# A two-block network on one core: four weight slots instead of three, split in place, and four pieces ahead of the norm's factor

## The chip, the cores and the metric

The kernel runs on one core of a Trainium2 chip. TensorE (PE) does the matrix products, ScalarE (ACT) and VectorE (DVE) the elementwise work, GpSimd (POOL) splits the weights into two parts, and SyncE (SP) only issues the weight loads. The metric is the device time of one execution in microseconds (us), lower is better.

## The reference, cut to what matters

Two blocks of two layers each work on the same 512 tokens of width 1024, all in float32.

```python
def rms_norm(x, g):                      # also _rmsnorm of the second block
    y = xf * lax.rsqrt(jnp.mean(xf * xf, axis=-1, keepdims=True) + RMS_EPS)
    return (y * g.astype(jnp.float32)).astype(x.dtype)

def first_block(x, ...):                 # x is 512 tokens x 1024
    for layer in range(2):
        h = rms_norm(x, norm_mix_pre[layer])
        if layer % 2 == 0:               # qkv: 1024 -> 9216, 3 groups of 8 heads, then 1024 -> 1024
            h = dilated_attention_mixer(h, attn_w_qkv[j], attn_w_o[j], rel_bias)
        else:                            # 1024 -> 2048, conv of 4 taps, gates, a scan over tokens, 1024 -> 1024
            h = rglru_mixer(h, lru_w_in[j], lru_conv_w[j], ..., lru_w_out[j])
        x = x + rms_norm(h, norm_mix_post[layer])
        h = rms_norm(x, norm_ffn_pre[layer])
        h = conv_ffn(h, ffn_w_up[layer], ffn_conv_w[layer], ffn_conv_b[layer], ffn_w_down[layer])
        x = x + rms_norm(h, norm_ffn_post[layer])
    return x

def conv_ffn(x, w_up, conv_w, conv_b, w_down):      # 1024 -> 6144 -> 3072 -> 1024
    u = causal_dwconv(x @ w_up, conv_w, conv_b)
    g, v = u[..., :D_FF], u[..., D_FF:]
    return (jax.nn.gelu(g, approximate=True) * v) @ w_down

def second_block(x, mem, norm_g, ...):
    for l in range(2):
        z = _rmsnorm(x, norm_g[l]) @ w_in[l]        # then split into the inputs of three branches
        o_a = _nsa(...) * silu(nsa_silu)            # compressed, selected and window attention
        o_b = _fox(...) * silu(fox_silu)
        o_m = _memory_xattn(mem_q, _rmsnorm(mem, mem_norm_g[l]) @ w_mem_kv[l], ...) * silu(mem_silu)
        u = sum over the three branches of sigmoid(merge_g) * (o @ w_branch)
        x = x + u @ w_out[l]
    return x
```

## The kernel before

**Weights.** All weights lie in memory as 434 units of 128 x 1024 floats (512 KB), in the order in which PE wants them (`unit_order`). A unit goes through three engines. SP loads it into `w_raw` of one of `SLOTS` slots. POOL rounds it into `w_hi` (L2002) and writes the rest, w_raw - w_hi, into `w_lo` in four quarters (L2006). PE then multiplies it in `pe_unit` (L355 to L357): 8 tiles, and for each tile w_hi by the high part of the activations, w_hi by their low part, and w_lo by the high part, which is 24 matmuls of 512 columns. Before the change there are three slots, each with its own `w_raw`, `w_hi` and `w_lo`. SP loads unit u as soon as POOL has split unit u-3 (L2016), and POOL splits unit u once it is loaded and PE has finished unit u-3 (L2001).

**Stages.** The program is a row of stages: the attention of the first block (its start runs on `order[0:3]`), the output projection `attn_out`, ffn 0, the recurrent stage (lru), ffn 1, and then, for two layers, the projections `z` of the second block, its attentions, and the merge. Six stages begin with a norm (`pe_norm_start`, L413): the activations enter unscaled, units 0 and 1 of the stage are multiplied together, chunk by chunk, as the chunks come from ACT and DVE, and PE sums the squares beside it (L393). After that DVE works out the norm's factor by twelve small instructions on 128x4 numbers (`dve_rsqrt`, L460 to L475), PE multiplies unit 2, and then PE spreads the factor over all partitions (`pe_norm_spread`, L408, L399), ACT copies it (L446, `factor_wide`), and only now can the banks of units 0, 1 and 2 be evicted by DVE, with the factor in the multiplication.

**Between stages.** Four stages (ffn 0, lru, ffn 1 and the first `z`) begin with the norm of what came before (`pe_post_begin`, L426): the last unit's bank is squared, PE sums it (L393), DVE finds the factor by the same twelve instructions into `narrow`, PE spreads it (L399), DVE scales eight chunks (L509), and POOL adds each to the residual `x_res` (`pool_post`, L520, L523). The place of `pool_post` in POOL's order is set by the table `post` in `pool_program` (L1996): it stands behind the split of unit SLOTS - 1 of the new stage.

**Order within a stage.** Each engine's order is written out by hand, and each waits on counters of the others. In lru, DVE has for each of eight units an eviction (L1007), three taps of the convolution (L1014) and the low part (L991), while PE goes on with the next units; the second group of gates waits for the eviction of the last one. In `z` the work beside unit m is listed by `later` (L1103): at m = 1 a rotation matmul (L1179) of what was evicted from unit 0, at m = 3 the gates' transposes (L1192), which want the eviction of unit 2 and a sigmoid.

## Time and profile before

| | us |
|---|---|
| median of 3 timed runs | 3247.79 |
| lowest and highest | 3241.72, 3254.14 |
| the profiled execution, its own time | 3239.93 |
| its span, from the first to the last instruction | 3238.5 |
| granted TensorE clock, mean of the span | 0.973 |

The profile is of one execution. Its span is the time between its first and last instruction, and 1.4 us of its own time lie outside. The busy time of PE is modelled from pipelined matmuls, so its share is no measure of how near PE is to its limit: idle time before an instruction, with what ended it, is read in its place. A clock of 1 is 2.4 GHz and 0.5 is 1.2 GHz.

### The profile page before, as it was taken

What the parts mean: (1) busy time and instruction counts of PE and PEld (TensorE: products, weight loads), DVE (VectorE), ACT (ScalarE), POOL (GpSimd) and SP (SyncE); (2) the same over time, 40 slices, a digit from 0 to 9 for tenths busy, and PEclk for the clock granted to TensorE, in tenths of its full rate; (3) what the DMA queues carried; (4) which work ended last, traced back from release to release, by engine and by line L of the source; (5) the groups of instructions that cost most, each with busy time, mean ns of one, the idle gap of its engine ahead of it and who ended that gap; (6) DMA issues with size and microseconds to landing.
All of it is one profiled execution on the core that took longest, in us unless ns stands there. A gap on an engine that the chain in (4) does not pass through costs nothing.

```text
span 3238.5 us, 41911 instructions
## 1 busy us (share of the span) xinstructions
PE 3068.2 (95%) x15410; PEld 2538.1 (78%) x15410; DVE 1541.2 (48%) x3162; ACT 820.7 (25%) x1763; POOL 1903.9 (59%) x2206
## 2 busy tenths in 40 slices
PE   7999999899998888999989999999999999999999
PEld 6888887678887667888877777778887787777887
DVE  2333334377721684777035745553233654655232
ACT  1111111222211342222012125553111213555110
POOL 5555554588877677898764751115775573111775
PEclk9999999899999999999999999999999999999999
DMA  3222221122222212222322220001233221000232
GB/s 143 89 92 83 90 101 59 53 91 98 98 98 85 65 65 73 97 98 98 110 92 98 85 78 21 27 21 66 98 117 107 70 89 55 27 22 26 85 98 91
DMA packets 66873, 255.71 MB, mean 79 GB/s; under 512 B 7664, under 2 KB 8176, under 8 KB 64880
## 3 DMA queue, kind: packets, MB, share of 16 engines
q1 hardware_dynamic: 62496, 227.57, 21.0%
q10 hardware_dynamic: 4176, 25.47, 2.2%
q8 instruction: 125, 2.05, 0.3%
q14 instruction: 76, 0.62, 0.1%
HBM read 250.91 MB, written 2.10 MB: 78 GB/s over the span
## 4 chain that ended last, share of the span: by engine, by line
PE 87%; DVE 8%; ACT 2%; issue 2%; DMA 0%; POOL 0%; ACTq 0%; DVEq 0%; POOLq 0%
PE bank L355 21%; PE bank L357 21%; PE bank L356 21%; PE bank L1692 4%; PE bank L1666 2%; PE bank L1677 2%; PE bank L393 2%; PE bank L383 1%; PE bank L621 1%; PE bank L1661 1%; PE bank L385 1%; PE bank L384 1%; PE bank L1424 1%; PE bank L593 1%; PE bank L1164 1%
## 5 line engine op out<-in xcount | busy, mean ns | idle before, releaser
L2006 POOL TENSOR_TENSOR w_lo<-w_raw,w_hi 128x256 fp32r<-128x256 f32 x1736 | 1383.6, 828 | 36.2
L2002 POOL TENSOR_SCALAR w_hi<-w_raw 128x1024 fp32r<-128x1024 f32 x434 | 474.9, 1094 | 1257.6 <-PE bank L357 1128.5
L355 PE MATMUL bank<-in_hi,w_hi 128*128 128x512 f32 x1408 | 555.6, 395 | 5.7 <-ACT factor_wide L446 2.8
L357 PE MATMUL bank<-in_hi,w_lo 128*128 128x512 f32 x1408 | 549.4, 390 | 0.0
L356 PE MATMUL bank<-in_lo,w_hi 128*128 128x512 f32 x1408 | 549.1, 390 | 0.0
L355 PE MATMUL bank<-z_hi,w_hi 128*128 128x512 f32 x976 | 394.5, 404 | 0.0
L357 PE MATMUL bank<-z_hi,w_lo 128*128 128x512 f32 x976 | 384.2, 394 | 0.0
L356 PE MATMUL bank<-z_lo,w_hi 128*128 128x512 f32 x976 | 383.6, 393 | 0.0
L355 PEld LDWEIGHTS bank<-in_hi,w_hi 128*128 128x128 f32 x1408 | 265.3, 188 | 59.9 <-ACT factor_wide L446 3.5
L357 PEld LDWEIGHTS bank<-in_hi,w_lo 128*128 128x128 f32 x1408 | 264.9, 188 | 55.5
L356 PEld LDWEIGHTS bank<-in_lo,w_hi 128*128 128x128 f32 x1408 | 265.3, 188 | 53.1
L357 PEld LDWEIGHTS bank<-z_hi,w_lo 128*128 128x128 f32 x976 | 185.2, 190 | 40.4
L355 PEld LDWEIGHTS bank<-z_hi,w_hi 128*128 128x128 f32 x976 | 185.7, 190 | 39.0 <-POOL w_lo L2006 1.0
L356 PEld LDWEIGHTS bank<-z_lo,w_hi 128*128 128x128 f32 x976 | 185.7, 190 | 38.7 <-issue 2.0
L1775 DVE TENSOR_REDUCE at_st<-bank 128x1 f32<-128x256 f32 (+4 forms) x288 | 118.7, 412 | 171.6 <-PE bank L1667 101.6
L575 DVE TENSOR_TENSOR out_squares<-out_squares,square 128x512 f32<-128x512 f32 x32 | 32.6, 1019 | 279.1 <-ACT square L566 279.0
L1705 ACT ACTIVATE at_pt<-bank 128x256 f32<-128x256 f32 (+4 forms) x288 | 112.2, 390 | 198.6 <-PE bank L1677 194.2
L355 PE MATMUL bank<-ffn_hidden_hi,w_hi 128*128 128x512 f32 x384 | 149.4, 389 | 0.0
L356 PE MATMUL bank<-ffn_hidden_lo,w_hi 128*128 128x512 f32 x384 | 149.4, 389 | 0.0
L357 PE MATMUL bank<-ffn_hidden_hi,w_lo 128*128 128x512 f32 x384 | 149.4, 389 | 0.0
L1677 PE MATMUL bank<-ident,at_p 128*128 128x128 f32 (+1 forms) x608 | 120.6, 286 | 24.2 <-ACT at_p L1712 23.8
L1712 ACT ACTIVATE at_p<-bank,at_st,nsa_scale 128x31 f32<-128x31 f32 (+2 forms) x192 | 103.2, 537 | 41.7 <-DVE at_st L1786 39.3
(427 smaller groups left out, 5157.2 us busy)
## 6 DMA issues: line engine op xcount, KB each, us to landing
w_raw<-in_units SPq DMA_DIRECT2D x434, 512.0 KB, 3.4
bias<-in_bias ACTq DMA_DIRECT2D x8, 1152.0 KB, 5.0
o_all<-in_cmp_w ACTq DMA_DIRECT2D x4, 2048.0 KB, 8.5
x_res<-in_x ACTq DMA_DIRECT2D x4, 512.0 KB, 9.0
mem_in<-in_mem ACTq DMA_DIRECT2D x2, 1024.0 KB, 4.8
out<-x_res ACTq DMA_DIRECT2D x4, 512.0 KB, 2.6
consts<-in_consts ACTq DMA_DIRECT2D x1, 710.5 KB, 3.7
both_layers_cols<-in_layer_cols ACTq DMA_DIRECT2D x2, 140.5 KB, 4.7
```

What stands on the lines that cost most here:

```text
L355: pe.matmul(out, hi[:, w], rh, start=start and n == 0, stop=False)
L356: pe.matmul(out, hi[:, w], rl, start=False, stop=False)
L357: last = pe.matmul(out, lo[:, w], rh, start=False, stop=stop and n == len(tiles) - 1)
L393: m = pe.matmul(bank[:, t:t + 1], sq[:, t * P:t * P + P], c.ones[:, 0:1], start=first and t == 0, stop=last, skip_group_check=True)
L1666: pe.matmul(b[:, 0:t.keys], c.nsa_q[:, t.n, q], k[:, 0:t.keys], start=True, stop=False)
L1677: m = pe.matmul(b[0:t.rows, s * P:s * P + P], p[:, s * P:s * P + t.rows], c.ident[:, :], is_transpose=True)
L1692: m = pe.matmul(o, pt[0:t.rows, s * P:s * P + P], v, start=s == 0, stop=s == len(values) - 1)
L1705: c.s.turned_out.on(act.activation(c.at_pt[t.index % 3][0:t.rows, 0:t.tiles * P], c.bank[3 + t.index % 2][0:t.rows, 0:t.tiles * P], ACT.Co ...
L1712: c.s.exponentials.on(act.activation(c.at_p[t.index % 3][:, 0:t.keys], c.bank[t.index % 3][:, 0:t.keys], ACT.Exp, scale=exp_scale(c, t), b ...
L1775: dmax = step.on(dve.reduce_max(st[:, 0:1], c.bank[t.index % 3][:, 0:t.keys], AX_X))
L2002: d = c.s.unit_hi.on(pool.tensor_scalar(c.w_hi[s][:, :], c.w_raw[s][:, :], 1.0, 0.0, ALU.mult, ALU.add))
L2006: last = pool.tensor_tensor(c.w_lo[s][:, w], c.w_raw[s][:, w], c.w_hi[s][:, w].bitcast(F32), ALU.subtract)
```

## The change

The number of slots goes from three to four. `w_lo` loses its own memory: it has the addresses of `w_raw`, so POOL writes the low part over the loaded weights, quarter by quarter. A slot's loaded weights are then in use until PE has finished the unit, so SP waits for PE (unit u-4) before it loads unit u, and POOL waits only for the load. `post` follows `SLOTS`, so `pool_post` now stands behind the split of the fourth unit of a stage. Five of the six starts (all but the first attention's) multiply four units before PE spreads the factor, and lru uses four banks in turn instead of three.

```diff
--- before.py
+++ after.py
@@ -19,7 +19,7 @@
 TT = T // P
 FC = 3 * D // P
 NEG = -1.0e30
-SLOTS = 3
+SLOTS = 4
 EPS = 1e-6
 
 HEADS = 8
@@ -171,10 +171,11 @@
     def __init__(self, nc, ctx, t):
         self.nc, self.t, self.s = nc, t, Signals(nc, ctx)
         self.bank = [ctx.enter_context(nc.psum_tensor(f"bank{b}", [P, T], F32)) for b in range(8)]
-        a = Area(nc, 1152)
+        first = 1536
+        a = Area(nc, first)
         self.w_raw = [a.take(f"w_raw{s}", [P, D]) for s in range(SLOTS)]
         self.w_hi = [a.take(f"w_hi{s}", [P, D], F32R) for s in range(SLOTS)]
-        self.w_lo = [a.take(f"w_lo{s}", [P, D], F32R) for s in range(SLOTS)]
+        self.w_lo = [Area(nc, first + 4 * D * s).take(f"w_lo{s}", [P, D], F32R) for s in range(SLOTS)]
         self.x = a.take("x_res", [P, DC, T])
         self.narrow = [a.take(f"narrow{j}", [P, 8]) for j in range(3)]
         self.ident, self.ones = a.take("ident", [P, P]), a.take("ones", [P, P])
@@ -418,7 +419,8 @@
         pe_norm_sum(pe, c, z, k)
     for _ in pieces:
         pass
-    pe_project(pe, c, keys[2], c.bank[2][:, :], z.hi, z.lo)
+    for b in range(2, len(keys)):
+        pe_project(pe, c, keys[b], c.bank[b][:, :], z.hi, z.lo)
     pe_norm_spread(pe, c, z)
     pe.wait_ge(*c.s.wide_ready[z.name])
 
@@ -851,10 +853,10 @@
 
 def pe_ffn(pe, c, layer, z, post):
     pe_post_begin(pe, c, post)
-    pe_norm_start(pe, c, z, [("up", layer, 0, 0), ("up", layer, 0, 1), ("up", layer, 1, 0)])
+    pe_norm_start(pe, c, z, [("up", layer, n, half) for n in range(2) for half in range(2)])
     for n in range(FC):
         for half in range(2):
-            if 2 * n + half < 3:
+            if 2 * n + half < 4:
                 continue
             if n >= 3:
                 pe.wait_ge(*c.s.evicted["up", layer, n - 3, half])
@@ -920,10 +922,10 @@
 
 def pe_lru(pe, c, z, post):
     pe_post_begin(pe, c, post)
-    pe_norm_start(pe, c, z, [("lru_in", n) for n in range(3)])
-    for n in range(3, DC):
-        pe.wait_ge(*c.s.evicted["lru_in", n - 3])
-        pe_project(pe, c, ("lru_in", n), c.bank[n % 3][:, :], z.hi, z.lo)
+    pe_norm_start(pe, c, z, [("lru_in", n) for n in range(4)])
+    for n in range(4, DC):
+        pe.wait_ge(*c.s.evicted["lru_in", n - 4])
+        pe_project(pe, c, ("lru_in", n), c.bank[n % 4][:, :], z.hi, z.lo)
     for b in range(4):
         banks = [c.bank[4 * ((b + 1) % 2) + q] for q in range(4)]
         pe.wait_ge(*c.s.lo_done["lru", 2 * b + 1, "conv"])
@@ -1004,7 +1006,7 @@
         dve.wait_ge(*c.s.unit_multiplied["lru_in", n])
         if n >= 2:
             dve.wait_ge(*step["conv", n - 2, 3])
-        c.s.evicted.on(dve.tensor_tensor(raw[:, :], c.bank[n % 3][:, :], z.wide, ALU.mult), ("lru_in", n))
+        c.s.evicted.on(dve.tensor_tensor(raw[:, :], c.bank[n % 4][:, :], z.wide, ALU.mult), ("lru_in", n))
         if n >= 1:
             dve_lru_parts(dve, c, n - 1)
         dve.wait_ge(*c.s.act_step["conv", n])
@@ -1134,11 +1136,11 @@
     every, groups = slots(c)
     compressed, memory = pe_compressed(pe, c, layer), pe_memory(pe, c, zm)
     c.free = {b: None for b in range(8)}
-    pe_norm_start(pe, c, z, [("z", layer, m) for m in range(3)])
+    pe_norm_start(pe, c, z, [("z", layer, m) for m in range(4)])
     for m in range(SLOTS_TWO + 1):
         if m < SLOTS_TWO:
             s = every[m]
-            if m >= 3:
+            if m >= 4:
                 pe_free(pe, c, m % 4)
                 if m == 11:
                     pe.wait_ge(*c.s.lo_done[zm.name, DC - 1])
@@ -1997,8 +1999,6 @@
     for u in range(len(c.order)):
         s = u % SLOTS
         pool.wait_ge(*c.s.unit_loaded[s][u])
-        if u >= SLOTS:
-            pool.wait_ge(*c.s.unit_multiplied[u - SLOTS])
         d = c.s.unit_hi.on(pool.tensor_scalar(c.w_hi[s][:, :], c.w_raw[s][:, :], 1.0, 0.0, ALU.mult, ALU.add))
         pool.wait_ge(*d)
         for quarter in range(4):
@@ -2013,7 +2013,7 @@
     for u in range(len(c.order)):
         s = u % SLOTS
         if u >= SLOTS:
-            sp.wait_ge(*c.s.unit_split[u - SLOTS])
+            sp.wait_ge(*c.s.unit_multiplied[u - SLOTS])
         c.s.unit_loaded[s].on(sp.dma_start(c.w_raw[s][:, :], c.t["units"][u]), u, 16)
 
 
```

On PE, at the start of layer 0 of the second block, these rows stand in order before (`z_factor_by_token` is the factor that is spread, `cmp_src_k` the rotated output of unit 0, `gate_cols_and_forget` that of unit 2; rows of unit 3 between are left out).

```order
L357 MATMUL bank2<-z_hi_135,w_lo2_57 128x512
L399 MATMUL bank6<-ident_62,z_factor_by_token_137 128x128 x4
L1179 MATMUL bank5<-cmp_src_k_173,consts_131 128x512
L355 MATMUL bank3<-z_hi_135,w_hi0_52 128x512
...
L357 MATMUL bank3<-z_hi_135,w_lo0_55 128x512
L1192 MATMUL bank4<-ident_62,gate_cols_and_forget_175 128x32 x4
L355 MATMUL bank0<-z_hi_135,w_hi1_53 128x512
```

And these in the changed kernel.

```order
L358 MATMUL bank2<-z_hi_138,w_lo2_59 128x512
L356 MATMUL bank3<-z_hi_138,w_hi3_56 128x512
...
L358 MATMUL bank3<-z_hi_138,w_lo3_60 128x512
L400 MATMUL bank6<-ident_65,z_factor_by_token_140 128x128 x4
L1181 MATMUL bank5<-cmp_src_k_176,consts_134 128x512
L1194 MATMUL bank4<-ident_65,gate_cols_and_forget_178 128x32 x4
L356 MATMUL bank0<-z_hi_138,w_hi0_53 128x512
```

The 24 matmuls of unit 3 (bank3) have moved from behind the spread and the rotation to ahead of them, so the rotation and the gates' transposes now stand next to each other.

On POOL, at the start of ffn 0, these are the last splits ahead of the residual additions before.

```order
L2002 TENSOR_SCALAR w_hi1_53<-w_raw1_50 128x1024
L2006 TENSOR_TENSOR w_lo1_56<-w_raw1_50,w_hi1_53 128x256 x4
L523 TENSOR_TENSOR x_res_58<-x_res_58,square0_72 128x512
```

And in the changed kernel.

```order
L2002 TENSOR_SCALAR w_hi2_55<-w_raw2_51 128x1024
L2006 TENSOR_TENSOR w_lo2_59<-w_raw2_51,w_hi2_55 128x256 x4
L2002 TENSOR_SCALAR w_hi3_56<-w_raw3_52 128x1024
L2006 TENSOR_TENSOR w_lo3_60<-w_raw3_52,w_hi3_56 128x256 x4
L525 TENSOR_TENSOR x_res_61<-x_res_61,square0_75 128x512
```

One more unit is split ahead of the additions; its load waits for the last unit of the stage before.

## Rows read from the trace of the kernel before

**Rows 1.** Head of the page.
```profile
span 3238.5 us, 41911 instructions
```

**Rows 2.** Waits of PE: us in total, times, longest us.
```profile
PE bank L399 <- DVE narrow L475: 13.3, 4, 3.4
...
PE bank L399 <- DVE factor_by_token L475: 8.2, 4, 2.1
...
PE bank L399 <- DVE z_factor_by_token L475: 4.4, 2, 2.3
PE bank L355 <- POOL w_lo L2006: 4.0, 1, 4.0
```

**Rows 3.** Tile w_raw: durations in ns (min/median/max) and DMA landing.
```profile
L2017 SPq DMA_DIRECT2D w_raw<-in_units x434: 327/328/424, 0.7 to 3209.9; - x145
...
DMA to landing us min/median/max: 3.3/3.4/8.4
```

**Rows 4.** Timeline, end of ffn 0: start us, us, engine, instruction, [idle before].
```profile
1029.56 1.05 POOL L2002 TENSOR_SCALAR w_hi<-w_raw 128x1024 fp32r<-128x1024 f32 x1 [1.48 <-PE bank L357]
...
1034.44 0.39 PE L357 MATMUL bank<-ffn_hidden_hi,w_lo 128*128 128x512 f32 x1
...
1034.99 1.05 POOL L2002 TENSOR_SCALAR w_hi<-w_raw 128x1024 fp32r<-128x1024 f32 x1 [1.48 <-PE bank L357]
...
1036.12 3.08 POOL L2006 TENSOR_TENSOR w_lo<-w_raw,w_hi 128x256 fp32r<-128x256 f32 x4
...
1037.72 0.16 DVE L460 TENSOR_SCALAR narrow<-bank 128x4 f32<-128x4 f32 x1 [1.15 <-PE bank L393]
1037.92 0.63 DVE L466 TENSOR_SCALAR narrow<-narrow 128x4 int32<-128x4 int32 x1
...
1039.26 0.16 DVE L471 TENSOR_TENSOR narrow<-narrow 128x4 f32<-128x4 f32 x1
...
1041.05 1.12 PE L399 MATMUL bank<-ident,narrow 128*128 128x128 f32 x4 [3.37 <-DVE narrow L475]
...
1043.04 8.82 POOL L523 TENSOR_TENSOR x_res<-x_res,square 128x512 f32<-128x512 f32 x6 [3.83 <-DVE square L509]
```

**Rows 5.** Timeline, start of the recurrent (lru) stage.
```profile
1066.23 0.16 DVE L460 TENSOR_SCALAR factor_tmp<-bank 128x4 f32<-128x4 f32 x1 [4.82 <-PE bank L393]
...
1068.80 1.05 POOL L2002 TENSOR_SCALAR w_hi<-w_raw 128x1024 fp32r<-128x1024 f32 x1
...
1068.89 0.97 DVE L475 SCALAR_TENSOR_TENSOR factor_by_token<-factor_tmp,factor_by_token 128x4 f32<-128x4 f32 x1
...
1075.13 0.69 DVE L1007 TENSOR_TENSOR lru_raw<-bank,factor_wide 128x512 f32<-128x512 f32 x1 [1.37 <-ACT factor_wide L446]
```

**Rows 6.** Timeline, the same stage where the gate units begin.
```profile
1116.60 0.68 DVE L1007 TENSOR_TENSOR lru_raw<-bank,factor_wide 128x512 f32<-128x512 f32 x1
...
1117.39 0.76 PE L355 MATMUL bank<-split_hi,w_hi 128*128 128x512 f32 x1 [7.86 <-issue]
```

**Rows 7.** Timeline, start of layer 0 of the second block.
```profile
1699.90 0.65 PE L399 MATMUL bank<-ident,z_factor_by_token 128*128 128x128 f32 x4 [2.07 <-DVE z_factor_by_token L475]
...
1702.10 2.04 PE L1179 MATMUL bank<-cmp_src_k,consts 128*128 128x512 f32 x2 [1.55 <-DVE cmp_src_k L1301]
...
1710.83 0.43 PE L1192 MATMUL bank<-ident,gate_cols_and_forget 32*128 32x32 f32 x4 [0.69 <-ACT gate_cols_and_forget L1245]
```

**Rows 8.** Timeline, the output projection of the first attention.
```profile
578.65 1.06 POOL L2002 TENSOR_SCALAR w_hi<-w_raw 128x1024 fp32r<-128x1024 f32 x1 [30.69 <-PE bank L385]
...
583.82 0.80 PE L355 MATMUL bank<-attn_o_hi,w_hi 128*128 128x512 f32 x1 [3.96 <-POOL w_lo L2006]
```

**Rows 9.** Windows: span, busy us of the engines, PEclk, DMA share, GB/s.
```profile
582.20:589.00 6.80, 5.18 (x12) 4.12 (x13) 0.31 (x1) 0.00 (x0) 6.63 (x9) 0.50 0.26 84
1701.70:1705.10 3.40, 3.00 (x5) 1.81 (x6) 1.17 (x3) 0.78 (x1) 1.00 (x2) 0.51 0.35 112
657.30:660.70 3.40, 2.85 (x7) 2.27 (x8) 1.95 (x3) 1.31 (x2) 2.03 (x3) 0.50 0.36 114
```

## The prediction

> **What bounds the kernel now.** I read the waits of PE first, then what stands before each of the longest in the timeline, and last the windows where PE's clock was low. The span is 3238.5 us [rows 1]. PE sets it in nearly all of it, so what counts is PE's idle time, and of that only what the slots and the starts can touch. The waits show four such items [rows 2]: the spread behind the norm's factor, 8.2 us in four starts (2.05 each) and 4.4 in two (2.07 and 2.34); the spread after a stage, waiting for `narrow`, 13.3 in four (3.3 each); and one wait of 4.0 for a split. PE waits for POOL only this once: the supply of weights is no bound. In the steady state a unit takes PE 5.43 us, the distance of two splits that each follow a finished unit (1029.56 and 1034.99) [rows 4].
>
> **The supply with four slots.** A load takes 3.4 us to land (up to 8.4) and costs SP 0.3 to issue [rows 3]; a split takes 1.05 + 3.1 us and some gap, about 4.2 [rows 4]. Before, a unit is ready 4.3 us after the one three places ahead is finished, with two units (10.9 us) in hand. After, it is ready 0.1 + 3.4 + 4.3 = 7.8 us after the one four places ahead, with three units (16.3 us) in hand. Even a load of 8.4 us leaves 3 us. So steady stretches neither win nor lose, and the sum is one of single places.
>
> **Attention's start** keeps its three pieces but loses the wait for the factor. The reason is in the start of lru: DVE's chain of twelve small instructions begins at 1066.23, and one of them takes 0.97 us where POOL's L2002 runs (1068.80) [rows 5]. In the other chain an instruction takes 0.63 while POOL's L2006 runs until 1039.20, and 0.16 once POOL is idle [rows 4]. So POOL's splits make this chain long: about 7.6 us (1066.23 to PE's spread at 1073.8, the eviction at 1075.13 less 1.3 for spread and copy) against twelve times 0.2 = 2.4 undisturbed. With four slots the split that follows units 0 and 1 starts a load later, by 3.4 us, when most of the chain is through. It then ends inside unit 2's 5.43 us. Gain 2.1.
>
> **attn_out.** Three units are multiplied together and free all three slots at once; the split of the fourth starts at 578.65 and PE waits 3.96 us for it [rows 8]. After, the fourth is there, so PE goes on at 579.9 and is done at 585.3. The fifth is loaded at 578.6 + 3.4 = 582.0 and split at 586.2 (by the 5.1 of the slow split between 578.65 and 583.8, at 587.2): a new wait of 0.9 to 1.9. Gain 2.1 to 3.1. The stretch 582.2 to 589.0 ran at a clock of 0.50, the lower level, after that wait [rows 9]; if it stays at the upper level another 3.4 us (half of 6.8) come back. Bounds 2.1 and 6.5; I take 4.5, the middle, since the shorter wait that stays is near neither.
>
> **The end of the four stages.** Here the change costs. Now the split that follows the last unit starts 0.55 us after that unit's last matmul (1034.44 to 1034.99), is done at 1039.20, and disturbs two instructions of DVE's chain (0.63 and the one behind it); from 1039.26 on each takes 0.16 and PE spreads at 1041.05 [rows 4]. After, that split waits for a load: it runs from 1034.99 + 3.4 = 1038.4 to 1042.6, over the whole rest of the chain. By 1038.4 three of the twelve are through (the first began at 1037.72, 0.2 each). Then one takes 0.97, and four or five more take 0.65 until 1042.6, the rest 0.2 each: 1038.4 + 1.0 + 4.5 x 0.68 + 3.5 x 0.2 = 1043.2, rounded by a last one that straddles the end to 1043.4. Against 1041.05 that is 2.4 us. The whole chain behind it (spread, scaling, additions, norm, first matmul) moves with it, and PE has nothing else. POOL itself isn't late: it is free at 1042.6, and its first addition, 1043.04 now, would come at 1045.4. Four stages x 2.4 = 9.6 lost. Bounds: 0, if the chain slips through ahead of the split, and 4.5 each (nine instructions at 0.65 in place of 0.16), so 18.
>
> The Trainium skill has the cause, in "GPSIMD Engine Reference", section "Specifications": the SBUF interfaces are shared with VectorE, with contention for instructions in a two-port mode or with two SBUF inputs. The trace agrees where it can be seen: the chain's first instruction reads PSUM and takes 0.16 us in both chains, with POOL at work in the second [rows 4, 5], the ones on SBUF 0.63 to 0.97. By that rule the evictions, with one SBUF input, cost the same wherever the split moves; without it they would be a further unknown.
>
> **The starts of ffn 0 and ffn 1.** PE bounds these stages, DVE has six banks to be late in. The spread behind four pieces finds the factor ready: 2 x 2.05 = 4.1 gained. The stretch at 657.3 after ffn 0's start ran 3.4 us at the lower level [rows 9]; if it doesn't, 1.7 more. I take 0.9.
>
> **The start of lru** is another matter. From the first eviction at 1075.13 DVE never waits for PE until the last at 1116.60 (its waits there are for ACT alone), and PE, long done, starts the gates at 1117.39 after 7.86 us idle [rows 5, 6]. What counts is when DVE begins, and that is behind PE's spread. A fourth piece puts 5.43 us ahead of it and takes away the wait of 2.05: 3.4 us lost, and none of PE's head start helps. The slow splits lie in DVE's stretch as before (the same six or so).
>
> **The starts of both z stages.** Before, unit 3 hides DVE's way from the spread to the gates' transposes: PE rotates at 1702.10 and reaches the transposes at 1710.83, only 0.69 late [rows 7]. After, unit 3 is ahead of the spread, so PE stands idle from about 1 us behind the rotation until DVE and ACT have evicted three units. The transposes come 10.9 us behind the spread in both kernels, and unit 4 behind them: lost again 5.43 - 2.07 = 3.4 and 5.43 - 2.34 = 3.1. POOL, idle in this stretch before, now splits: two DVE instructions at 1.1 in place of 0.7, 0.8 each. An idle time of some 7 us will bring the lower level for longer than the 3.4 us that were there at 1701.7 [rows 9]; one such stretch more costs 1.7 each. Together 3.4 + 3.1 + 1.6 + 3.4 = 11.5.
>
> **The sum.** -2.1 - 4.5 + 9.6 - 4.1 - 0.9 + 3.4 + 11.5 = +12.9 us. On the profiled execution's own 3239.9 that is 3253; this execution was 8 us below the median of the three timed runs, 3247.8, so I add the sum to the median: 3260.
>
> **Rivals.**
> - *The splits don't disturb the ends of the stages.* The chain is mostly through, or the instructions on 128x4 numbers are slow for another reason than POOL. For it: three of twelve are through anyway. Against: 0.63 and 0.16 on either side of the split's end. Then 12.9 - 9.6 = +3.3: 3251. Chance 0.15.
> - *The fourth piece costs nothing where DVE is the bound.* DVE catches up in lru and z, each start gives its 2.1 back, and the ends still lose: -12.6 - 4.5 - 1.7 + 9.6 = -9: 3239. For it: DVE's taps vary with POOL's splits. Against: DVE never waits for PE in lru. Chance 0.10.
> - *Faster.* The waits simply go: six for the factor (12.6), attn_out's with its clock (up to 6.5), and nothing is added, since load and split are hidden by the three units in hand at the ends of stages too: -19, 3229. It decides if DVE's small instructions stay at 0.16 there and z's transposes come as soon after the spread as PE is free. Chance 0.07.
> - *Clock and contention both worse.* PE's longer idle times at four ends and three starts each bring one more stretch of 3.4 us at the lower level (1.7 each, 12) and the ends lose nearer 4 than 2.4 (+6): +30, 3278. Chance 0.13.
>
> My forecast has 0.55, with a range of its own from 3250 to 3270. The range over all cases that leaves two in ten out is 3238 to 3277. A change of 0.5% is 16 us, about what can be told from none: slower by more takes the worst case and a third of the forecast's, 0.33; faster by more only the faster rival, 0.08; within it 0.59.
>
> **What would show it.** In the changed profile PE's waits for `factor_by_token` and `z_factor_by_token` are gone (also at attention's start), and that for `narrow` grows from 3.3 to about 5.7 each, with POOL's split running from 4 us after the last matmul. In attn_out the 3.96 us for POOL become 1 to 2. PE's idle time before lru's second gates grows from 7.9 to some 14, and before z's transposes from 0.7 to 6 or more. I am wrong if `narrow`'s wait stays at 3.3, if the transposes come sooner than 10 us behind the spread, or if PE waits for splits in steady stretches.

## The result, and the profile after

| | us |
|---|---|
| changed kernel, median of 7 runs | 3258.20 (3253.12 to 3266.95) |
| kernel before beside it, median of 7 runs | 3246.25 (3240.67 to 3254.14) |
| ratio, 95% interval | 1.0044 [1.0029, 1.0059] |
| profiled execution of the changed kernel | 3265.76, span 3264.3 |

The change costs 0.44% here, some 14 us by the ratio (12 by the medians), where 12.9 were forecast. The two profiled executions lie 25.8 us apart, since the profile of before fell below its median and this one above. So the pair of profiles shows where waits moved, and the runs show how much it came to. Three executions in the runs below took 3684, 7835 and 16294 us, in a slow state, and no ratio has them.

The waits of PE in the changed kernel (us in total, times, longest us) answer to [rows 2].

```profile
PE bank L400 <- DVE narrow L477: 20.8, 4, 5.5
PE bank L1194 <- ACT gate_cols_and_forget L1247: 13.8, 2, 6.9
PE bank L356 <- issue: 12.8, 2, 12.3
...
PE bank L356 <- DVE ffn_hidden_lo L912: 1.8, 1, 1.8
...
PE bank L356 <- POOL w_lo L2006: 1.0, 1, 1.0
```

The waits for the factor, 12.6 us in six, are gone, and the 4.0 for a split in attn_out are 1.0. Against that stand 7.5 us more for `narrow` and 13.1 more for the gates' sigmoid in z. The 1.8 for `ffn_hidden_lo` is new, and I had not thought of it.

The timeline at the end of ffn 0 answers to [rows 4]: start us, us, engine, instruction, [idle before].

```profile
1022.64 0.17 DVE L470 TENSOR_SCALAR narrow<-narrow 128x4 int32<-128x4 int32 x1
1022.79 1.04 POOL L2002 TENSOR_SCALAR w_hi<-w_raw 128x1024 fp32r<-128x1024 f32 x1 [1.11 <-DMA w_raw<-in_units]
1022.85 0.99 DVE L473 TENSOR_TENSOR narrow<-narrow 128x4 f32<-128x4 f32 x1
1023.87 0.16 DVE L475 SCALAR_TENSOR_TENSOR narrow<-narrow,narrow 128x4 f32<-128x4 f32 x1
1023.91 2.76 POOL L2006 TENSOR_TENSOR w_lo<-w_raw,w_hi 128x256 fp32r<-128x256 f32 x4
...
1024.69 0.65 DVE L473 TENSOR_TENSOR narrow<-narrow 128x4 f32<-128x4 f32 x1
...
1026.05 0.65 DVE L477 SCALAR_TENSOR_TENSOR narrow<-narrow,narrow 128x4 f32<-128x4 f32 x1
1026.73 0.16 DVE L473 TENSOR_TENSOR narrow<-narrow 128x4 f32<-128x4 f32 x1
...
1027.34 1.11 PE L400 MATMUL bank<-ident,narrow 128*128 128x128 f32 x4 [5.14 <-DVE narrow L477]
```

Four instructions on 128x4 numbers fall under `L2006` and take 0.58 to 0.65, the one under `L2002` takes 0.99, and the others 0.16 or 0.17 (six of the twelve are left out here). POOL's split starts because a load has landed, no longer because a unit is finished.

In this execution PE stays at the lower level (0.50) after the spread longer than in that of before. The windows give span, busy us of PE, PEld, DVE, ACT and POOL, PEclk, DMA share and GB/s: first the kernel before, at the starts of lru, ffn 1 and z, then the changed kernel at the same places.

```profile
1039.60:1049.80 10.20, 4.78 (x16) 3.81 (x16) 8.02 (x17) 3.20 (x5) 6.76 (x5) 0.50 0.16 51
1247.80:1258.00 10.20, 4.53 (x14) 3.55 (x15) 7.99 (x18) 3.19 (x5) 6.50 (x5) 0.50 0.15 51
1664.20:1677.90 13.70, 8.52 (x28) 6.99 (x28) 11.53 (x20) 7.37 (x12) 10.54 (x7) 0.50 0.12 39
```

```profile
1024.60:1048.50 23.90, 17.20 (x56) 14.48 (x56) 13.23 (x21) 6.93 (x11) 13.39 (x12) 0.50 0.00 1
1243.00:1266.90 23.90, 16.79 (x54) 14.10 (x54) 13.64 (x21) 6.93 (x11) 13.79 (x12) 0.50 0.00 1
1662.90:1680.00 17.10, 8.48 (x27) 6.96 (x28) 14.79 (x24) 7.37 (x12) 14.17 (x12) 0.50 0.00 1
```

PE's wait for `narrow` ahead of these stretches grew by 1.9 us on average, and the stretches by 13.7, 13.7 and 3.4. At the start of ffn 0 it is the other way, 13.7 us from 604.7 on where before had 20.5 from 616.3 on. That the one makes the other is not shown: the kernel before with the additions earlier (below), where that wait is 2.5 us and not 3.3, has stretches of 20.5, 13.7 and 23.9 us at the same places. The first of them:

```profile
1040.20:1060.70 20.50, 16.54 (x54) 13.82 (x54) 10.87 (x14) 6.93 (x11) 14.12 (x11) 0.50 0.00 1
```

The start of z answers to [rows 7], and the gates of lru to [rows 6].

```profile
1707.31 1.10 PE L1181 MATMUL bank<-cmp_src_k,consts 128*128 128x512 f32 x2 [1.50 <-DVE cmp_src_k L1303]
1715.22 0.63 PE L1194 MATMUL bank<-ident,gate_cols_and_forget 32*128 32x32 f32 x4 [6.81 <-ACT gate_cols_and_forget L1247]
```

```profile
1110.72 0.68 DVE L1009 TENSOR_TENSOR lru_raw<-bank,factor_wide 128x512 f32<-128x512 f32 x1
...
1111.51 0.76 PE L356 MATMUL bank<-split_hi,w_hi 128*128 128x512 f32 x1 [12.29 <-issue]
```

### The profile page after: what moved, and what is told of

It reads as the page before. It is cut to its first block, busy times and chain, and to the rows that moved or that the text cites. A ratio compares the mean times of both kernels' runs of the same rounds, so it can differ in the third digit from the quotient of the medians.

```text
span 3264.3 us, 41479 instructions
## 1 busy us (share of the span) xinstructions
PE 3085.2 (95%) x15410; PEld 2553.9 (78%) x15410; DVE 1497.1 (46%) x3162; ACT 820.7 (25%) x1763; POOL 1909.3 (58%) x2206
## 4 chain that ended last, share of the span: by engine, by line
PE 80%; DVE 11%; ACT 4%; issue 4%; DMA 0%; POOL 0%; ACTq 0%; DVEq 0%
PE bank L356 19%; PE bank L358 19%; PE bank L357 19%; PE bank L1694 4%; PE bank L1668 2%; PE bank L1679 2%; PE bank L394 2%; PE bank L384 1%; PE bank L623 1%; PE bank L1663 1%; PE bank L386 1%; PE bank L385 1%; DVE ffn_raw L903 1%; PE bank L1426 1%; DVE ffn_v L910 1%
## 5 line engine op out<-in xcount | busy, mean ns | idle before, releaser
L2006 POOL TENSOR_TENSOR w_lo<-w_raw,w_hi 128x256 fp32r<-128x256 f32 x1736 | 1379.7, 825 | 36.2
L2002 POOL TENSOR_SCALAR w_hi<-w_raw 128x1024 fp32r<-128x1024 f32 x434 | 484.5, 1116 | 1279.2 <-DMA w_raw<-in_units 1278.2
L1679 PEld LDWEIGHTS bank<-ident,at_p 128*128 128x128 f32 (+1 forms) x608 | 70.8, 144 | 55.8 <-ACT at_p L1714 33.7
```

The lines of the kernel that those rows point to most:

```text
L1679: m = pe.matmul(b[0:t.rows, s * P:s * P + P], p[:, s * P:s * P + t.rows], c.ident[:, :], is_transpose=True)
L2002: d = c.s.unit_hi.on(pool.tensor_scalar(c.w_hi[s][:, :], c.w_raw[s][:, :], 1.0, 0.0, ALU.mult, ALU.add))
L2006: last = pool.tensor_tensor(c.w_lo[s][:, w], c.w_raw[s][:, w], c.w_hi[s][:, w].bitcast(F32), ALU.subtract)
```

## The experiments

The kernel before ran beside each batch, with a median of 3246.2 to 3246.8, so the ratios can be set side by side. "Four" and "three" are the pieces ahead of the spread.

| kernel | slots | pieces | median us | ratio to before, 95% |
|---|---|---|---|---|
| changed | 4 | four | 3258.20 | 1.0044 [1.0029, 1.0059] |
| three pieces | 4 | three | 3243.47 | 0.9988 [0.9972, 1.0005] |
| slots undone | 3 | four | 3281.32 | 1.0096 [1.0077, 1.0115] |
| changed, three in z | 4 | four, three in z | 3261.59 | 1.0051 [1.0033, 1.0070] |
| two pieces in lru and z | 4 | two or three | 3255.45 | 1.0017 [1.0002, 1.0031] |
| changed, additions earlier | 4 | four | 3254.49 | 1.0029 [1.0013, 1.0046] |
| three pieces, additions earlier | 4 | three | 3248.87 | 0.9997 [0.9980, 1.0014] |
| before, additions earlier | 3 | three | 3247.33 | 1.0000 [0.9987, 1.0014] |
| before, longer split | 3 | three | 3259.26 | 1.0043 [1.0030, 1.0056] |
| three pieces, PE kept busy | 4 | three | 3230.62 | 0.9954 [0.9936, 0.9971] |
| before, PE kept busy | 3 | three | 3231.24 | 0.9957 [0.9944, 0.9969] |
| changed, PE kept busy | 4 | four | 3249.81 | 1.0004 [0.9991, 1.0018] |
| three, earlier, kept busy | 4 | three | 3232.02 | 0.9964 [0.9949, 0.9978] |

### The two halves of the change apart

Three pieces ahead of each spread, with four slots (lru keeps its four banks):

```diff
-        for b in range(2, len(keys)): pe_project(...)      # units 2 and 3, then the spread
+    pe_norm_start(pe, c, z, [("lru_in", n) for n in range(3)])   # and so in ffn and z
```

> The four slots as changed, but every stage multiplies three units ahead of the spread, as before. Theory (a fourth piece delays DVE where DVE sets the end): lru gets back 5.4 us and each z start 5.4 us and about 1.5 of clock, the ffn starts and attention's start stay as they are, since the factor is found inside the third unit anyway; 19 us under the changed kernel and 5 under the one before, ratio to before 0.998. No wait for factor_by_token or z_factor_by_token, narrow still 5.2 each. Rival (the fourth piece costs nothing, the loss is all in the ends of stages): as the changed kernel, 1.004.

Slots undone, four pieces kept:

```diff
-SLOTS = 4
+SLOTS = 3                      # w_lo with memory of its own, and the waits of before
```

> Three slots with their own low parts as before, but four pieces ahead of the spread in five starts. Theory: the ffn starts win 2 us each, lru loses 3.4 and the z starts lose 3 to 5 each; 8 us over before, ratio 1.0025, waits for narrow at 3.3 each. Rival (the slots bring the whole loss, the fourth piece only takes waits away): the five waits for the factor go and nothing comes, 10 us under before, 0.997.

The waits of PE, first with three pieces and four slots, then with four pieces and three slots:

```profile
PE bank L400 <- DVE narrow L477: 20.9, 4, 5.6
...
PE bank L1195 <- ACT gate_cols_and_forget L1248: 5.0, 2, 2.5
```

```profile
PE bank L356 <- DVE ffn_hidden_lo L912: 15.4, 2, 7.7
...
PE bank L1194 <- ACT gate_cols_and_forget L1247: 13.7, 2, 6.8
PE bank L400 <- DVE narrow L477: 13.3, 4, 3.4
...
PE bank L356 <- POOL w_lo L2008: 4.0, 1, 4.0
```

The timeline of the second at the end of ffn 0's `up` units:

```profile
887.18 1.15 DVE L912 TENSOR_TENSOR ffn_hidden_lo<-ffn_v,ffn_hidden_hi 128x512 fp32r<-128x512 f32 x1 [0.70 <-ACT ffn_hidden_hi L883]
...
898.06 1.15 DVE L912 TENSOR_TENSOR ffn_hidden_lo<-ffn_v,ffn_hidden_hi 128x512 fp32r<-128x512 f32 x1 [0.70 <-ACT ffn_hidden_hi L883]
...
908.94 1.15 DVE L912 TENSOR_TENSOR ffn_hidden_lo<-ffn_v,ffn_hidden_hi 128x512 fp32r<-128x512 f32 x1 [0.70 <-ACT ffn_hidden_hi L883]
...
918.88 0.69 DVE L912 TENSOR_TENSOR ffn_hidden_lo<-ffn_v,ffn_hidden_hi 128x512 fp32r<-128x512 f32 x1 [0.69 <-ACT ffn_hidden_hi L883]
919.62 0.80 PE L356 MATMUL bank<-ffn_hidden_hi,w_hi 128*128 128x512 f32 x1 [7.70 <-DVE ffn_hidden_lo L912]
```

The separation of the mechanisms holds. `narrow`'s wait goes with the slots (20.9 with four, 13.3 with three), whatever the pieces; the wait for the sigmoid goes with the pieces. Three pieces did come out at the 0.998 expected, even with the kernel before. The second run missed its 1.0025 widely, by some 23 us. Its waits show 15.4 of them: at the first `down` unit of each ffn PE waits 7.7 us for `ffn_hidden_lo`, with nothing of the kind before. The rest comes with 55 us more at the lower level in the mean (249 against 194, see below), and its cause was not separated. Four pieces put one more of PE's units ahead of DVE's evictions, and with three slots it never makes up for it: two units take it 10.88 us (887.18, 898.06, 908.94), which is PE's own pace of 5.43 each. Its lag, from the end of a unit on PE to the start of that unit's eviction, is 16 to 17 us at the third unit with four pieces and 11 to 13 with three. At the last unit but one it is 14.3 here, 7.2 and 4.1 in the two ffn stages of the changed kernel, 3.4 before, and 1.4 with four slots and three pieces. That the pace is set by which of DVE's instructions POOL's split falls on fits their durations (the convolution's taps take 0.75, 1.1 or 1.4 us at the same shape) but was not tested by itself.

### The fourth piece in z alone

```diff
-    pe_norm_start(pe, c, z, [("z", layer, m) for m in range(4)])
+    pe_norm_start(pe, c, z, [("z", layer, m) for m in range(3)])     # ffn and lru keep four
```

> The changed kernel with three pieces ahead of the spread in the two z stages alone; ffn and lru keep four. Theory (z is where the fourth piece costs most: some 3 + 3 us of schedule, and most of the changed kernel's extra time at the lower clock, 95 us in the two z stages against 48 before): 3260 less 6 and less 0.38 x 45 = 17, about 3240, even with the run that has three pieces everywhere (3243). Rival (the clock's part is not tied to z's idle time): 3253. PE's wait for gate_cols_and_forget 5 instead of 13.8 in both.

```profile
PE bank L400 <- DVE narrow L477: 20.4, 4, 5.6
...
PE bank L1194 <- ACT gate_cols_and_forget L1247: 4.2, 2, 2.5
PE bank L356 <- DVE ffn_hidden_lo L912: 3.5, 2, 2.0
```

The wait for the sigmoid shrinks from 13.8 to 4.2, and the time does not: 1.0051 against 1.0044. My theory falls, and so does the rival with its 3253. The fourth piece costs nothing in z that can be seen here, where the intervals leave some 8 us either way. Between this kernel and the one with three pieces everywhere only ffn and lru differ, and there lies all of the distance of 0.63%, about 20 us. Of these, 3.5 us are waits for `ffn_hidden_lo`.

### Two units ahead of the spread in lru and z

```diff
+    pe_norm_start(pe, c, z, [("lru_in", n) for n in range(2)])
+    pe_norm_start(pe, c, z, [("z", layer, m) for m in range(2)])
```

> Four slots, three pieces in the ffn starts, but only two units ahead of the spread in lru and in both z starts. Theory (in lru and z the end is set by when DVE can begin to evict): DVE begins 3 us earlier than with three pieces, since its chain takes 2.4 us without a split beside it, PE waits 2.4 for the factor, and 3 us come back at each of three starts: 9 us under e1, ratio to before 0.996. Rival (PE's own waits are what counts): each of the three starts gains a wait of 2.4 for the factor, 7 us over e1, 1.001.

```profile
PE bank L400 <- DVE z_factor_by_token L477: 6.5, 2, 3.3
...
PE bank L400 <- DVE factor_by_token L477: 2.4, 1, 2.4
```

A miss, and the rival came out: DVE begins sooner, but PE waits again for the factor. By the ratios, three pieces are better by 0.3%. A part of that goes with the clock (216 us at the lower level in the mean, against 199).

### The end of the stages

Two edits shorten the chain behind `narrow`, in the kernels with four and three slots: `pool_post` moves ahead by one split, so that none falls between the last unit and the additions.

```diff
-    post = {c.order.index(key) + SLOTS - 1: name for key, name in begins.items()}
+    post = {c.order.index(key) + SLOTS - 2: name for key, name in begins.items()}
```

> The changed kernel with the residual additions one split earlier in POOL's order, behind the third unit of the new stage, so that POOL waits idle while DVE's twelve small instructions run. Theory (POOL's split beside the chain makes it long): the wait for narrow falls from 5.2 to 2.4 each, below the 3.3 of before; 11 us under the changed kernel, ratio to before 1.001. Rival (the chain is slow for another reason): the wait for narrow stays at 5.2 and the time too, 1.004.

> Four slots, three pieces ahead of the spread, and the additions behind the third split. Theory: both repairs add up, 19 + 11 us under the changed kernel, 16 us under before, ratio 0.995. Rival (fourth piece harmless): only the 11 us of the additions, 1.001. Rival (chain not disturbed by POOL): only the 19, 0.998.

> The kernel before (three slots) with the residual additions behind the second split of the new stage instead of the third. Theory (a split beside DVE's small instructions lengthens them): the two slow instructions of the chain go, the wait for narrow falls from 3.3 to 2.4 each, 4 us under before, ratio 0.999. Rival: the wait stays at 3.3 and the time is the same.

The row for `narrow` in these three kernels, in this order:

```profile
PE bank L400 <- DVE narrow L477: 10.2, 4, 2.9
```

```profile
PE bank L400 <- DVE narrow L477: 9.9, 4, 2.6
```

```profile
PE bank L399 <- DVE narrow L475: 9.8, 4, 2.5
```

And one that lengthens it: the kernel before, with the low part of that split written twice (the second time into the same place).

```diff
+        if u in post:
+            for quarter in range(4):
+                last = pool.tensor_tensor(c.w_lo[s][:, w], c.w_raw[s][:, w], c.w_hi[s][:, w].bitcast(F32), ALU.subtract)
```

> The kernel before, where POOL writes the low part of one unit (the third of each of the four new stages) a second time with the same values, 3.1 us more of POOL's work beside DVE's chain at the end of a stage, and nothing else. Slots, loads and pieces are untouched. Theory: the wait for narrow grows from 3.3 to about 5.5 each, as in the changed kernel, and the time by 8 us, ratio 1.0025. Rival (the longer chain there has to do with slots or loads): the wait stays at 3.3, and the time the same, since POOL is free before its first addition.

```profile
PE bank L399 <- DVE narrow L475: 20.9, 4, 5.2
...
PE bank L355 <- DVE ffn_hidden_lo L910: 3.6, 1, 3.6
```

Shown: a split beside the chain sets `narrow`'s wait, 9.8 us with none, 13.3 as it was [rows 2], and 20.9 with a longer one, in one kernel and with the same slots, loads and pieces. Lengthening it cost more than the 7.6 us of the wait (14 by the ratio): 3.6 of wait for `ffn_hidden_lo` came with it, and 21 us more at the lower level in the mean (215 against 194).

Shortening it paid less than it gave back in waits, and the expected times of the first two runs were missed (1.001 and 0.995). In the changed kernel it gave 10.6 us of waits and 5 by the ratio, whose interval overlaps that of the changed kernel. With three pieces it gave 11.0 of waits and nothing (0.9997 against 0.9988), and in the kernel before 3.5 of waits and nothing, where the interval leaves room for the 4 expected. In all three the mean time at the lower level went up, by 14, 20 and 11 us. So the wait is explained, but what taking it away is worth in time is not: a good part seems to come back as clock, and no run shows why.

### The clock

From the time t and the mean clock c of an execution, the time at the lower level is 2(1 - c)t, between 135 and 268 us. Over 194 executions of 14 kernels, each taken against its own kernel's mean, t grows by 0.37 us for each us at the lower level, with a correlation of 0.89. So what one kernel scatters by (some 0.3%) goes mostly with this. The means are 194 us at the lower level before (78 runs), 219 changed, 199 with three pieces, 227 with three in z alone, 249 with the slots undone, and with the additions earlier 232 (changed), 219 (three pieces) and 205 (before). Four sets of extra matmuls test whether that share can be had by itself: PE multiplies `ident` by itself into a bank that is overwritten later, and nothing reads it.

```diff
+    for _ in range(8):          # 5 in the kernel with the additions earlier
+        pe.matmul(c.bank[0][:, 0:P], c.ident[:, :], c.ident[:, :], start=True, stop=True)
     pe.wait_ge(*c.s.factor_found["post", name])
     pe_spread(pe, c, c.bank[6], c.narrow[0], TT, ("post", name))
+    for _ in range(12):
+        pe.matmul(c.bank[0][:, 0:P], c.ident[:, :], c.ident[:, :], start=True, stop=True)
```

> As e1 (four slots, three pieces), with 8 extra matmuls of 128 columns into a free bank while PE waits for narrow and 12 while it waits for the first chunk of the new stage; their output is never read. Theory (part of what the ends of stages cost, and most of the spread between executions, is the lower clock after PE's idle time): the time at the lower level at the four ends falls from some 100 us in e1's profile by half or more, and the kernel wins half of that, less about 1 us each for matmuls in the way: 15 us under e1, ratio to before 0.994. Rival (the clock does not matter there, since DVE and POOL set the pace of these stretches): same as e1 or a little slower, 0.999 to 1.001.

> Three pieces ahead of every spread and pool_post behind the third split (as in the run with both edits), and beside that 5 matmuls of 128 columns ahead of narrow's spread and 12 behind it, whose result nothing reads. Theory (the time is the schedule plus about 0.38 us for each us at the lower clock): the run with both edits had 219 us at the lower level and was even with the kernel before; kept busy, it should have some 150, so about 25 us less: 3222, ratio 0.992; narrow's wait of PE about 5. Rival (the extra matmuls only pay where the gap they fill is long; with the additions earlier it is not): 3235 or more, no faster than the run with three pieces and extra matmuls (3230).

> The changed kernel with 8 matmuls of 128 columns ahead of narrow's spread and 12 behind it, whose result nothing reads. Theory (two thirds of the change's loss is clock lost behind longer idle times of PE at the ends of stages and at z, a third is schedule): about 3247, 11 us or more under the changed kernel, and the distance to the kernel before with the same extra matmuls stays near 10, since z's idle time is not filled. Rival (the loss is all schedule, the clock falls as often in both): the distance stays 14 and both lose or win the same few us.

> The kernel before with the same 8 and 12 extra matmuls, whose result nothing reads. Theory: its low-clock time falls from about 196 us to some 150, so 15 us less: 3232, ratio 0.9955. Rival (its idle time behind narrow is 3.3 us and too short to cost clock): 3245 to 3250, the matmuls in the way of the spread cost what they bring.

The timeline of the kernel before with them, at the end of ffn 0 (the profile has two rows for each of these matmuls of 128 columns):

```profile
1032.37 3.63 PE L431 MATMUL bank<-ident 128*128 128x128 f32 x16
1035.86 0.65 PE L399 MATMUL bank<-ident,narrow 128*128 128x128 f32 x4
1036.35 2.84 PE L435 MATMUL bank<-ident 128*128 128x128 f32 x24
1040.48 0.50 PE L383 MATMUL bank<-in_hi,w_hi 128*128 128x512 f32 x1 [1.29 <-DVE in_lo L455]
1040.81 0.40 PE L384 MATMUL bank<-in_lo,w_hi 128*128 128x512 f32 x1
```

The first matmul of lru's norm takes 0.50 and the next 0.40. Without the extra work the same first one took 0.79 at the lower level, after 3.96 us of idle time:

```profile
1046.13 0.79 PE L383 MATMUL bank<-in_hi,w_hi 128*128 128x512 f32 x1 [3.96 <-DVE in_lo L451]
```

The extra work is worth 14 us in the kernel before (0.9957 [0.9944, 0.9969], about as expected), and, by the ratios, 11 with three pieces and 13 in the changed kernel. The mean time at the lower level fell by 47, 38 and 39 us, which at 0.37 each would be 17, 14 and 14: the slope, which comes from the scatter of each kernel, holds roughly for a change of the program too. My expectation that the distance between changed and before would fall to 10 was wrong: by the ratios it is 15 (1.0004 against 0.9957), as the rival had it. So the changed kernel's extra time at the lower level is not the one that these matmuls fill; with them it still has 180 us against 147.

The candidate for the best, all three edits, came out at 3232.0 where 3222 were expected, nearer to the rival's 3235: it has 175 us at the lower level, not 150. The kernel is no better than the kernel before with the extra matmuls alone, 3231.2, which beats both kernels of this study, by the smallest edit.

## Why the prediction was right or wrong

The time was near, 3258.2 for 3260, and the mechanism of the second largest term, the ends of the stages, was as described. That the sum fits so well is luck: what was forecast of waits and order was too dear, what was forecast of the clock too cheap, and the two made up for each other.

- **The ends of the four stages** (+9.6, 2.4 each). Right in mechanism. By the waits it is 7.5, 1.9 each: beside `L2006` four slow instructions, as forecast or one fewer, and one of 0.16 came between. The run that lengthened the split and those that moved the additions show the cause of the wait. The rival by which splits don't disturb the chain is out. The section "Specifications" of "GPSIMD Engine Reference" in the Trainium skill has the SBUF interfaces shared with VectorE. The trace agrees, with 0.16 beside an idle POOL and 0.58 to 0.99 beside `L2006` and `L2002`.
- **attn_out** (-4.5). The wait went from 3.96 to 1.0, and the stretch at 0.50 is gone, as the two windows of 582.2 to 589.0 show [rows 9]. In the changed kernel:

```profile
582.20:589.00 6.80, 6.80 (x31) 5.63 (x30) 0.84 (x1) 1.09 (x2) 6.72 (x9) 1.00 0.22 77
```

  By the starts of PE's units the stage is 3.6 us shorter. (The middle of the bounds 2.1 and 6.5 is 4.3, not 4.5, and 12.9 on 3247.8 is 3260.7; neither changes anything.)
- **Attention's start** (-2.1). The wait is gone. The two profiles differ by 8.2 us there. Some 4 of them are of the execution and not of the change (last section). The other 4 are more than the wait: the kernel with both edits, whose PE took up its faster pace at 26.43 as the one before did at 26.54, is 4.4 us sooner there. The kernel before has 6.8 us at the lower level from 46.3 on, and that one none.
- **ffn 0 and ffn 1** (-5.0). This is the step that failed: "PE bounds these stages, DVE has six banks to be late in." The waits for the factor are gone, and their price was right: with some 2.5 us at the lower level in both, the `up` units take 271.1 us in the changed kernel (ffn 0) and 273.3 in the one before (ffn 1). The stretch of 3.4 us at the lower level behind ffn 0's start is gone too. But the banks don't make the lateness free. At the end of the `up` units PE wants the last hidden part, and whatever DVE is behind by then is paid there: 1.8 us in the profile of the changed kernel, 3.5 with three in z, and 15.4 with the slots undone. What the six banks hide is only what DVE makes up for in the stage, and that this hangs on where POOL's splits fall was not tested.
- **lru's start** (+3.4). The idle time before the gates grew from 7.86 to 12.3, less than the 14 forecast. Here "none of PE's head start helps" was too strong. DVE takes 40.4 us from its first eviction to its last (1070.34 to 1110.72), where it took 41.5 before and 43.6 with four slots and three pieces. So of the 3.4 forecast 1.1 come back, and by these profiles a fourth piece costs lru 2.2 us, not 5.4. By the starts of PE's units the stage lost 5.8 us up to its output projection and 8.6 up to the last unit of it in the profiled pair, but most of the stretch of 23.9 us at 0.50 is in that, where before had 10.2.
- **z** (+11.5). The rotation now stands 8 us ahead of the transposes and PE waits 6.8 us, as forecast. But the run with three in z shows no gain, so 11.5 were hardly lost. A part of the answer is in PE's unit starts: from unit 2 to unit 3 it is 5.5 us less and from unit 3 to unit 4 8.0 more, a net 2.5 in layer 0 and 2.1 in layer 1, not 3.4 and 3.1. The transposes come 10.0 and 10.1 us behind the spread (1705.21 to 1715.22 in layer 0), where before had 10.9 and 11.2 and the forecast took 10.9 for both. Why even the 2.5 and 2.1 can't be seen in the time was not settled; the uncertainty of that comparison is about 8 us.
- **The clock** (-0.9, +3.4, and -1.7 at attn_out) was mis-sized. The forecast has 0.8 us of it in sum. The mean over all runs has 25 us more at the lower level than before (by the scatter, 12 to 38), which at 0.37 each is 9 us, so about two thirds of the 14 lost. The rival "clock and contention both worse" had that cause for 12 us at four ends and three starts. It was right in that the clock got worse, and the z loss that it took over from the forecast was not seen.

The terms as the profiled pair shows them, without the clock, are -2.1 for attention's start, -3.0 for attn_out, +7.5 for the ends, -4.1 and +1.8 for the ffn stages, +2.3 for lru and +4.6 for z: +7.0, where 12.1 were forecast. With 9 for the clock that is 16, against the 14 measured. This is an account and not a test, and its weakest terms are z's and the clock's.

What fits the runs together: four slots with three pieces win nothing (0.9988, interval across 1). By the waits, 7.5 us more for `narrow` eat the starts and attn_out; but taking the wait for `narrow` down as well won nothing either. The fourth piece in ffn and lru costs 18 to 20 us by the ratios, with some 6 or 7 of uncertainty. Of these, 2 to 4 are a wait for `ffn_hidden_lo`, and 2.2 are lru's later start. It comes with 20 to 27 us more at the lower level in the mean (219 and 227 against 199), 7 to 10 us at 0.37 each. The remaining 5 to 7 weren't located, nor was it shown why the clock is lower longer in these kernels.

## What to carry to other kernels

A deeper buffer moves the moment at which work starts, and with it the shared resource that it takes: look at what short chain now runs beside it. A wait that goes is not yet time that is won: three edits took 3.5 to 11 us of waits away, and the runs gave back 0 to 5. Buffers that let a consumer be late only hide what it makes up for before the next hard wait; compare its lag at the start and at the end of the stage. Idle time of PE can cost more than itself when the clock falls behind it, and where a chain must be waited for, a few matmuls that nothing reads were worth more (0.43% here, [0.31, 0.56]) than any re-ordering tried here.

## What the runs showed of the hardware

**PE starts slow in a way that the clock's column does not show.** At the start of the program matmuls of 512 columns take 0.63 us and follow each other every 0.43, as they do in the windows given as 0.50 above (in the changed kernel at 1033.01 and 1033.43, for one); at some point they change to 0.39 and 0.23. The first at the faster pace, in the kernel before, the changed one and the one with three in z:

```profile
26.54 0.48 PE L383 MATMUL bank<-in_hi,w_hi 128*128 128x512 f32 x1
```

```profile
18.10 0.48 PE L384 MATMUL bank<-in_hi,w_hi 128*128 128x512 f32 x1
```

```profile
30.98 0.48 PE L384 MATMUL bank<-in_hi,w_hi 128*128 128x512 f32 x1
```

The same stretch in the windows of before and after, where the clock is given as 1.00 in both, with 26 matmuls recorded in the one and 43 in the other:

```profile
17.00:24.00 7.00, 7.00 (x26) 6.13 (x26) 0.75 (x1) 2.12 (x4) 0.58 (x1) 1.00 0.39 141
```

```profile
17.00:24.00 7.00, 7.00 (x43) 6.27 (x42) 1.67 (x2) 3.67 (x6) 4.68 (x6) 1.00 0.00 0
```

The packed traces say why the column is silent. Their first clock record comes at 25.8 us in the kernel before, at 17.6 in the changed one and at 30.6 in the one with three in z, less than 1 us ahead of the first matmul at the faster pace. So it is in all 14 traces. Ahead of it there is no record, and a stretch without one is printed as 1.00. The pace there is that of the lower level, and neither the mean clock nor the times at the lower level above count this stretch.

The changed kernel and the one with three in z have the same code there, and 12.9 us at half the pace are up to 6.4 us of time. In the pair of before and after, half of 8.4 us is 4.2 of the 8.2 by which attention's start differed: luck of one execution, and a reason not to read a start out of a single profile.

**A small instruction of DVE ends with the POOL instruction beside it.** One on 128x4 numbers takes 0.16 us alone and up to six times as much beside POOL. The times show that it waits for the end of the POOL instruction that is running. In the changed kernel's timeline above, `L2002` ends at 1023.83 and the DVE instruction beside it at 1023.84. The four quarters of `L2006` end at 1024.64, 1025.32, 1026.00 and 1026.68, and DVE's four slow instructions at 1024.65, 1025.34, 1026.02 and 1026.70. In the 14 traces 491 instructions on 128x4 numbers in SBUF start beside a running split instruction, and 487 of them end 3 to 31 ns after it. The 52 that read PSUM all take 0.16. So what a chain loses goes by the length of the POOL instructions beside it, up to 0.5 us for a quarter of 0.72 and up to 0.8 for `L2002` with its 1.04, for each instruction of the chain that one falls on.

Large instructions lose somewhat less in us, and much less as a share: a tap on 128x510 takes 0.75 beside an idle POOL and 1.10 to 1.12 where `L2006` runs all along. In ffn 0 of the kernel before (tile `ffn_raw`, durations in ns min/median/max), a tap takes 1.41 in the median and 0.75 at the least, and the eviction, which reads PSUM, keeps its 0.68:

```profile
L901 DVE TENSOR_TENSOR ffn_raw<-bank,factor_wide x45: 675/679/683, 660.9 to 895.2; 128x512 f32<-128x512 f32 x45
...
L905 DVE SCALAR_TENSOR_TENSOR ffn_g<-ffn_raw,taps,ffn_g x23: 750/1410/1418, 660.2 to 893.8; 128x510 f32<-128x510 f32 x23
```

**A lag can hold itself.** With three slots DVE keeps PE's pace at three different lags: 3.4 us behind it in the second half of both ffn stages (three pieces), 8.8 in ffn 0 of the kernel with the longer split, and 14.3 with four pieces. PE pays 3.6 us for the second and 7.7 in each ffn for the third. With four slots the same late start was made up for to 7.2 and 4.1 us. Which of DVE's instructions a split falls on would explain that, and was not tested.
